# Low weight products last in every chunk, and the second block's gate products, sums and splits in another order

## The chip, the cores and the metric

One core of a Trainium2 chip runs the whole program, a single launch. The metric is the device time of that launch in microseconds. TensorE (PE) multiplies, VectorE (DVE), ScalarE (ACT) and GpSimd (POOL) work on tiles in SBUF and PSUM, and SyncE (SP) issues the DMA transfers of the weights.

## What is computed

Two blocks, each with two layers, on 256 tokens of width 1024, all in fp32. Cut to its frame:

```python
def first_block(h, ...):
    for l in range(2):
        proj = rms_norm(h, norm1_w[l]) @ w_in[l]
        z, xbc, dt_f, dt_b, sc_b, sc_c, sc_v = split(proj)
        mix = concat([ssd_branch(z, xbc, dt_f, dt_b, ...), sc_b * dwconv(sc_c * sc_v)])
        h = h + mix @ w_out[l]
        n = rms_norm(h, norm2_w[l])
        gate, up = split(dwconv(n @ w_ffn_up[l]) + ffn_conv_b[l])
        h = h + (silu(gate) * up) @ w_ffn_down[l]          # 2 x 2816 columns up
    return rms_norm(h, final_norm_w)

def second_block(x, ...):
    for l in range(2):
        u_conv, dq, dk, dv, mq, mk, mv, g = split(x @ w_in[l])
        y_a = conv_branch(u_conv, ...)           # 31-wide conv, layer norm, silu, @ w_conv_out
        y_b = diff_attention(dq, dk, dv, ...)    # ... @ w_diff_out
        y_c = moba_attention(mq, mk, mv, ...)    # ... @ w_moba_out
        gates = sigmoid(g + b_gate[l])
        m = gates[0] * y_a + gates[1] * y_b + gates[2] * y_c
        x = layer_norm(alpha * x + m @ w_o[l], ...)
        h = relu(x @ w_ff1[l] + b_ff1[l]) ** 2   # 4096 columns
        x = layer_norm(alpha * x + h @ w_ff2[l] + b_ff2[l], ...)
    return x
```

## The kernel before

Every large product is fp32 made of three products of rounded parts (fp32r): a weight is `whi + wlo`, an input `xh + xl`, and the kernel adds whi·xh, whi·xl and wlo·xh in PSUM. The weights are cut into chunks of 1 MB (half as much in a few). SP loads chunk after chunk into `raw`, which has three slots. ScalarE rounds it into `whi` in two halves (`split_hi`, L1095, semaphore `hi_done`); it first waits until the chunk two before has been multiplied (`chunk_done`). VectorE subtracts, again in two halves (`split_lo`, L1527, semaphore `w_ready`), and TensorE multiplies.

Three kinds of chunk matter. A *plain* chunk (`gemm`, L504 to L506) has 48 products of 256 columns: for every tile of weights the three products stand in a row. A *wide* chunk (the FFN's way up, `gemm_wide`, L549 and L550) has 16 pairs: one product of 512 columns, whi with both input parts side by side, and one of 256, wlo with the high input part. A *down* chunk (`down_pass`, L607 to L609, and its like for the mix's and the attention's way out, L579 to L581) has 24 products of 512 columns, in which the weights stream and the hidden tile stands: high × high, high × low weights, low hidden × high weights, again three in a row into one PSUM bank. In the FFNs a down chunk stands behind two wide ones in the first block and behind one in the second. `weights(c, cx, half)` waits for `w_ready` of that half ahead of its first product of any kind.

In front of each of the four layers' two matrix stages stands a norm. Its result comes out tile by tile: ScalarE writes the high part (L1147), VectorE the low one (L1616, L1605 in the first block), and the first chunk behind the norm takes the tiles as they come (`gemm_paced`, or `gemm_wide` with `base`), waiting for `n_ready`, the low part, of each. Down chunks wait for `hid_ready`, the low part of the hidden tile (L1876 in the first block).

In the second block chunks 28 to 31 are the outputs of the diff-attention and conv branches and chunks 32 to 35 those of the MoBA branch. VectorE multiplies each with its gate out of PSUM (`gated`, L2070; L2101 in the loop over q), GpSimd adds the products of chunks 30 and 31 into `macc` (L1073, two SBUF inputs), VectorE adds those of 32 to 35 (L2103), ScalarE halves and rounds the sum (L1481) and VectorE makes its low part (L2107), the input of chunks 36 and on (L579 to L581, w_o). Each engine has one queue in program order, and this order is written out by hand.

## Time and profile before

| | us |
|---|---|
| median of three runs | 1733.12 |
| lowest, highest | 1733.06, 1733.71 |
| the profiled execution, its own time | 1733.45 |
| its span in the trace | 1731.6 |
| TensorE busy | 1698.5 (98%) |
| VectorE busy | 1331.9 (77%) |
| ScalarE busy | 961.3 (56%) |
| GpSimd busy | 60.2 (3%) |

The granted TensorE clock has a mean of 0.998 of full speed. Busy time is a share of the span; the matmuls overlap, so one of 256 columns has a record of 0.28 us though the next begins 0.12 us after it. What a product costs is therefore read from the distance of starts, and where TensorE stands still from its list of waits. A row of the timeline has the start, the duration (of all in a folded row), engine, line, operation and tiles, and in brackets the idle time ahead and who ended it.

### The profile page before, as it was taken

The numbers are of one execution on the slowest core, as the hardware profiler recorded it, in microseconds if no ns is written. First come the engines' busy times: TensorE is split into PE (matmuls) and PEld (weight loads), VectorE is DVE, ScalarE is ACT, GpSimd is POOL, SyncE is SP. The second block draws the span as 40 slices with busy tenths as digits, with TensorE's granted clock in tenths as the row PEclk, the third lists the DMA queues.
The fourth block names the chain that finished last, engine by engine and source line by source line (L and its number), as shares of the span: only waits on it lengthen the run. The fifth ranks groups of instructions, "written<-read, shape, count | busy, mean of one in ns | idle before, by whom it ended". The sixth has DMA issues, their size and how long they took to land.

```text
span 1731.6 us, 27884 instructions
## 1 busy us (share of the span) xinstructions
PE 1698.5 (98%) x11152; PEld 1514.4 (87%) x11152; DVE 1331.9 (77%) x2074; ACT 961.3 (56%) x1584; POOL 60.2 (3%) x81
## 2 busy tenths in 40 slices
PE   8999999999999999999999999999999999999998
PEld 7999888888999988888899998788879999978886
DVE  6867678888877758878799888766678988886666
ACT  5566556565656656655645654544454476454443
POOL 1000000000200000000000001000000000100001
PEclk9999999999999999999999999999999999999999
DMA  7544545555545446555466454555546645455552
GB/s 217 164 146 147 170 163 182 191 194 158 171 146 148 146 160 204 195 187 184 162 199 194 147 171 150 197 185 188 193 149 216 195 146 172 135 194 195 192 186 84
DMA packets 233006, 299.71 MB, mean 173 GB/s; under 512 B 6163, under 2 KB 198317, under 8 KB 232877
## 3 DMA queue, kind: packets, MB, share of 16 engines
q1 hardware_dynamic: 232569, 297.82, 53.2%
q8 instruction: 88, 1.44, 0.3%
q14 instruction: 41, 0.34, 0.1%
q10 hardware_dynamic: 308, 0.12, 0.0%
HBM read 292.67 MB, written 1.05 MB: 170 GB/s over the span
## 4 chain that ended last, share of the span: by engine, by line
PE 82%; DVE 13%; ACT 2%; issue 2%; POOL 0%; DVEq 0%; ACTq 0%; POOLq 0%
PE ring_banks L549 16%; PE ring_banks L504 9%; PE ring_banks L505 9%; PE ring_banks L506 9%; PE ring_banks L550 8%; PE bank L607 5%; PE bank L608 5%; PE bank L609 5%; DVE weights_lo L1527 5%; PE ring_banks L579 2%; PE ring_banks L581 2%; PE ring_banks L580 2%; PE bank L729 1%; DVE conv_sums L1933 1%; PE ring_banks L634 1%
## 5 line engine op out<-in xcount | busy, mean ns | idle before, releaser
L1527 DVE TENSOR_TENSOR weights_lo<-raw_weights,weights_hi 128x1024 fp32r<-128x1024 f32 (+1 forms) x552 | 648.3, 1215 | 115.5 <-ACT weights_hi L1095 114.3
L1095 ACT ACTIVATE weights_hi<-raw_weights 128x1024 fp32r<-128x1024 f32 (+1 forms) x552 | 544.3, 1037 | 201.8 <-PE bank L609 95.1
L504 PE MATMUL ring_banks<-input_parts,weights_hi 128*128 128x256 f32 x1568 | 450.5, 287 | 10.3 <-DVE weights_lo L1527 4.0
L505 PE MATMUL ring_banks<-input_parts,weights_hi 128*128 128x256 f32 x1568 | 444.2, 283 | 0.0
L506 PE MATMUL ring_banks<-input_parts,weights_lo 128*128 128x256 f32 x1568 | 444.1, 283 | 0.0
L549 PE MATMUL ring_banks<-input_parts,weights_hi 128*128 128x512 f32 x1184 | 420.3, 398 | 4.0 <-DVE input_parts L1616 3.3
L550 PE MATMUL ring_banks<-input_parts,weights_lo 128*128 128x256 f32 x1184 | 332.0, 280 | 0.0
L504 PEld LDWEIGHTS ring_banks<-input_parts,weights_hi 128*128 128x128 f32 x1568 | 301.1, 192 | 16.0 <-issue 13.3
L505 PEld LDWEIGHTS ring_banks<-input_parts,weights_hi 128*128 128x128 f32 x1568 | 301.3, 192 | 0.1
L506 PEld LDWEIGHTS ring_banks<-input_parts,weights_lo 128*128 128x128 f32 x1568 | 301.2, 192 | 0.0
L549 PEld LDWEIGHTS ring_banks<-input_parts,weights_hi 128*128 128x128 f32 x1184 | 222.3, 188 | 60.2 <-issue 3.7
L550 PEld LDWEIGHTS ring_banks<-input_parts,weights_lo 128*128 128x128 f32 x1184 | 223.5, 189 | 1.8
L607 PE MATMUL bank<-weights_hi,hidden_hi 128*128 128x512 f32 x432 | 169.4, 392 | 1.1 <-DVE hidden_lo L1876 1.1
L608 PE MATMUL bank<-weights_lo,hidden_hi 128*128 128x512 f32 x432 | 168.6, 390 | 0.0
L609 PE MATMUL bank<-weights_hi,hidden_lo 128*128 128x512 f32 x432 | 168.4, 390 | 0.0
L1933 DVE SCALAR_TENSOR_TENSOR conv_sums<-conv_padded,params_second_layer,conv_sums 128x256 f32<-128x256 f32 x240 | 98.8, 478 | 0.0
L607 PEld LDWEIGHTS bank<-weights_hi,hidden_hi 128*128 128x128 f32 x432 | 81.1, 188 | 19.9 <-DVE hidden_lo L1876 1.9
L609 PEld LDWEIGHTS bank<-weights_hi,hidden_lo 128*128 128x128 f32 x432 | 81.1, 188 | 17.8
L608 PEld LDWEIGHTS bank<-weights_lo,hidden_hi 128*128 128x128 f32 x432 | 81.1, 188 | 15.1
L1495 ACT ACTIVATE pair<-ring_banks,params_second_layer 128x256 f32<-128x256 f32 x64 | 26.9, 471 | 106.2 <-PE ring_banks L550 106.2
L2139 DVE TENSOR_TENSOR pair<-ring_banks,pair 128x512 f32<-128x512 f32 x32 | 22.1, 691 | 75.7 <-ACT pair L1495 75.7
L579 PE MATMUL ring_banks<-weights_hi,hidden_hi 128*128 128x512 f32 x192 | 75.9, 395 | 1.5 <-DVE weights_lo L1527 1.5
(272 smaller groups left out, 2161.6 us busy)
## 6 DMA issues: line engine op xcount, KB each, us to landing
raw_weights<-in_w_in SPq DMA_DIRECT2D x104, 1024.0 KB, 5.3
raw_weights<-in_w_ff SPq DMA_DIRECT2D x64, 1024.0 KB, 5.3
raw_weights<-in_w_ffn_up SPq DMA_DIRECT2D x44, 1024.0 KB, 5.0
raw_weights<-in_w_ffn_down SPq DMA_DIRECT2D x22, 1024.0 KB, 4.9
raw_weights<-in_w_out SPq DMA_DIRECT2D x16, 1024.0 KB, 5.1
raw_weights<-in_w_o SPq DMA_DIRECT2D x8, 1024.0 KB, 5.1
pair<-pair SPq DMA_DIRECT2D x64, 64.0 KB, 2.8
raw_weights<-in_w_diff_out SPq DMA_DIRECT2D x4, 1024.0 KB, 5.1
```

Of the source, the lines that this page charges most:

```text
L504: mm(o, w_hi, x_hi, start=first, stop=False, skip_group_check=quiet)
L505: mm(o, w_hi, x_lo, start=False, stop=False, skip_group_check=quiet)
L506: return mm(o, w_lo, x_hi, start=False, stop=last, skip_group_check=quiet)
L549: mm(b[:, :], wh, inputs[:, k, :, :].rearrange("p a t -> p (a t)"), start=first, stop=last, skip_group_check=True)
L550: return mm(b[:, 0:SEQ], wl, nh[:, k, :], start=False, stop=last, skip_group_check=True)
L579: mm(banks[t][:, :], x_h, w_h, start=opens and k == 0, stop=False)
L607: mm(o, x_h, whi[:, s, r], start=first, stop=False)
L608: mm(o, x_h, wlo[:, s, r], start=False, stop=False)
L609: return mm(o, x_l, whi[:, s, r], start=False, stop=last)
L1095: A(whi[:, t, i * n:(i + 1) * n], raw[:, s, i * n:(i + 1) * n], ACT.Copy).then_inc(hi_done, 1)
L1527: tt(wlo[:, t, r], raw[:, s, r], whi[:, t, r].bitcast(f32), SUB).then_inc(w_ready, 1)
L1933: ins = stt(out=cacc[:, k, :], in0=src, scalar=w, in1=cacc[:, k, :], op0=MUL, op1=ADD)
```

## The change

In every chunk the products with high weights now come first and wait for `hi_done` only; those with low weights follow and wait for `w_ready`. In a plain chunk that is 32 products, then 16. A wide chunk has its 16 products of 512 columns, then its 16 of 256. A down chunk has 8 of high × high (waiting for `hid_hi`, the hidden tile's high part), 8 of low hidden × high weights (`hid_ready`), and 8 with low weights; consecutive products go to different banks. At a norm the first chunk waits for `n_hi`, and the products of the low input part stand two tiles behind; a wide chunk at a norm becomes 48 products of 256 columns. SP's queue is as before.

In the second block `gate_product` of chunk 30's first half moves between the two conv activations. The products of chunk 31 go to two further buffers, and GpSimd's sums wait for `chunk_done` of chunk 31 (m = 0, 1) and 32 (m = 2, 3). VectorE waits for the sums' first half ahead of the q loop and for the rest at q = 2. The low split of chunk 36 is cut in two around q2's product, that of chunk 37 stands ahead of q3's product (it stood behind it), and ScalarE splits chunk 37 ahead of its wait for q3's sum.

```diff
-            def passes(o, w_hi, w_lo, x_hi, x_lo, first, last, quiet=False):
-                mm(o, w_hi, x_hi, start=first, stop=False, skip_group_check=quiet)
-                mm(o, w_hi, x_lo, start=False, stop=False, skip_group_check=quiet)
-                return mm(o, w_lo, x_hi, start=False, stop=last, skip_group_check=quiet)
-            def weights(c, cx, half):
+            def high(c, cx, half):
+                pe.wait_ge(hi_done, cx * 2 + (2 * c + half + 1))
+            def low(c, cx, half):
                 pe.wait_ge(w_ready, (cx + c) * 2 + (2 * RAW + 1 + half))
...
+            def add(o, w, x, first=False, last=False):
+                return mm(o, w, x, start=first, stop=last, skip_group_check=True)
+            def gemm(c, cx, u, ux, o, nk, n, xh, xl, x0=0):
                 if u is not None:
                     pe.wait_ge(ring_free, ux + u + 1)
...
+                for i in range(2):
+                    high(c, cx, i)
+                    for m in range(n // P):
+                        for k in range(i * nk // 2, (i + 1) * nk // 2):
+                            wh, wl = tile(c, k * n + m * P)
+                            add(target(m), wh, xh[:, x0 + k, :], k == 0 and m % 2 == 0)
+                            add(target(m), wh, xl[:, x0 + k, :])
+                for i in range(2):
+                    low(c, cx, i)
+                    for m in range(n // P):
+                        for k in range(i * nk // 2, (i + 1) * nk // 2):
+                            wh, wl = tile(c, k * n + m * P)
+                            last = add(target(m), wl, xh[:, x0 + k, :], False, k == nk - 1)
                 last.then_inc(chunk_done, 1)
...
+            def gemm_paced(c, cx, freed, left, right, base):
+                pe.wait_ge(ring_free, freed)
+                def by_low_input(i):
+                    k = TRANSPOSED[i]
                     pe.wait_ge(n_ready, base + (i + 1))
                     for m in range(2):
                         wh, wl = tile(c, k * 256 + m * P)
+                        last = add(right[m], wh, nl[:, k, :], False, i == 7)
+                    return last
+                for i, k in enumerate(TRANSPOSED):
+                    if i % 4 == 0:
+                        high(c, cx, i // 4)
+                        low(c, cx, i // 4)
+                    pe.wait_ge(n_hi, base + (i + 1))
+                    for m in range(2):
+                        wh, wl = tile(c, k * 256 + m * P)
+                        add(left[m], wh, nh[:, k, :], i == 0 and (m == 0 or right is not left))
+                        add(left[m], wl, nh[:, k, :])
+                    if i >= 2:
+                        by_low_input(i - 2)
+                by_low_input(6)
+                by_low_input(7).then_inc(chunk_done, 1)
+            def gemm_wide(c, cx, freed, v):
+                pe.wait_ge(ring_free, freed)
+                for i in range(2):
+                    high(c, cx, i)
+                    for m in range(2):
+                        for k in range(4 * i, 4 * i + 4):
+                            wh, wl = tile(c, k * 256 + m * P)
+                            add(wide_bank(v, m), wh, inputs[:, k, :, :].rearrange("p a t -> p (a t)"), k == 0)
+                for i in range(2):
+                    low(c, cx, i)
+                    for m in range(2):
+                        for k in range(4 * i, 4 * i + 4):
+                            wh, wl = tile(c, k * 256 + m * P)
+                            last = add(wide_bank(v, m)[:, 0:SEQ], wl, nh[:, k, :], False, k == 7)
                 last.then_inc(chunk_done, 1)
...
+            def wide_paced(c, cx, freed, v, base):
+                parts = [[wide_bank(v, m)[:, i * SEQ:(i + 1) * SEQ] for m in range(2)] for i in range(2)]
+                gemm_paced(c, cx, freed, parts[0], parts[1], base)
...
+                def by_high(k, t):
+                    o, x_h, x_l, w_h, w_l = parts(k, t)
+                    add(o, x_h, w_h, opens and k == 0)
+                    add(o, x_l, w_h)
+                if first_tokens is None:
+                    for i in range(2):
+                        high(c, cx, i)
+                        for t in range(TOK):
+                            by_high(2 * i, t)
+                            by_high(2 * i + 1, t)
+                    for i in range(2):
+                        low(c, cx, i)
+                        for t in range(TOK):
+                            by_low(2 * i, t)
+                            last = by_low(2 * i + 1, t)
...
+            def down(c, cx, t0, opens, n):
+                places = [(t, half) for t in range(TOK) for half in range(2)]
+                pe.wait_ge(hid_hi, n)
                 for kk in range(2):
...
+                    high(c, cx, kk)
+                    for t, half in places:
+                        o, x_h, x_l, w_h, w_l = down_parts(c, t0, kk, t, half)
+                        add(o, x_h, w_h, opens and kk == 0)
+                pe.wait_ge(hid_ready, n)
+                for kk in range(2):
+                    for t, half in places:
+                        o, x_h, x_l, w_h, w_l = down_parts(c, t0, kk, t, half)
+                        add(o, x_l, w_h)
+                for kk in range(2):
+                    low(c, cx, kk)
+                    for t, half in places:
+                        o, x_h, x_l, w_h, w_l = down_parts(c, t0, kk, t, half)
+                        last = add(o, x_h, w_l)
+                last.then_inc(chunk_done, 1)
+            def down_last(c, cx, t0, n):
+                pe.wait_ge(hid_hi, n)
+                for kk in range(2):
+                    high(c, cx, kk)
+                    for half in range(2):
+                        o, x_h, x_l, w_h, w_l = down_parts(c, t0, kk, 0, half)
+                        add(o, x_h, w_h)
...
                     pool.wait_ge(ring_free, l * U2 + (UB2 + U2_OUT + 4 + m + RING + 1))
+                    if m % 2 == 0:
+                        pool.wait_ge(chunk_done, l * C2 + (CB2 + 31 + m // 2 + SPL + 1))
                     x = macc[:, 2 * m:2 * m + 2, :]
-                    nc.gpsimd.tensor_tensor(x, x, tmp[m % 2][:], ALU.add).then_inc(pool_added, 1)
+                    product = tmp[(0, 1, 3, 4)[m]]
+                    nc.gpsimd.tensor_tensor(x, x, product[:], ALU.add).then_inc(pool_added, 1)
...
                         split_hi(34 + q, cx, cr, columns(list2, 34 + q))
+                    else:
+                        split_hi(37, cx, cr)
                     act.wait_ge(mp_ready, l * 4 + q + 1)
                     A(hidh[:, 2 * q:2 * q + 2, :], macc[:, 2 * q:2 * q + 2, :], ACT.Copy, scale=0.5).then_inc(mp_hi, 1)
-                split_hi(37, cx, cr)
...
+                def gate_product(c, m):
+                    first = c < 30
+                    j = c - 28 if first else c - 30
+                    u = U2_OUT + 2 * (c - 28) + m
+                    k = 4 * j + 2 * m
+                    g = gates[:, (8 if first else 16) + k:(10 if first else 18) + k, :]
+                    o = macc[:, k:k + 2, :] if first else tmp[m + 3 * j][:]
+                    stt(out=o, in0=g, scalar=1.0, in1=pair(ring[u % RING]), op0=ADD, op1=MUL).then_inc(ring_free, 1)
                 def gated(c):
                     multiplied(c, cx)
                     for m in range(2):
+                        gate_product(c, m)
                     split_lo(c + 2, cx, n=columns(list2, c + 2))
                 gated(28)
                     x = cacc[:, 2 * q:2 * q + 2, :]
                     dve.wait_ge(cth, l * 2 + q + 1)
                     stt(out=x, in0=tmp[3 + q][:], scalar=1.0, in1=x, op0=ADD, op1=MUL).then_inc(cact, 1)
+                    if q == 0:
+                        multiplied(30, cx)
+                        gate_product(30, 0)
                 for q in range(2):
                     dve.wait_ge(chi, l * 2 + q + 1)
                     t = slice(8 + 2 * q, 10 + 2 * q)
                     tt(hidl[:, t, :], cacc[:, 2 * q:2 * q + 2, :], hidh[:, t, :].bitcast(f32), SUB).then_inc(conv_ready, 1)
-                gated(30)
+                gate_product(30, 1)
+                split_lo(32, cx, n=columns(list2, 32))
+                dve.wait_ge(cact, l * 2 + 2)
+                gated(31)
                 dve.wait_ge(pool_added, l * 4 + 2)
-                gated(31)
-                dve.wait_ge(pool_added, l * 4 + 4)
                 for q in range(4):
                     c, u = 32 + q, U2_OUT + 8 + q
                     multiplied(c, cx)
+                    if q == 2:
+                        split_lo(36, cx, halves=(0,))
+                        dve.wait_ge(pool_added, l * 4 + 4)
+                    if q == 3:
+                        split_lo(37, cx)
                     x = macc[:, 2 * q:2 * q + 2, :]
                     stt(out=tmp[q % 2][:], in0=gates[:, 2 * q:2 * q + 2, :], scalar=1.0, in1=pair(ring[u % RING]), op0=ADD, op1=MUL).then_inc(ring_free, 1)
                     dve.wait_ge(ring_free, ux + (u + RING + 1))
                     tt(x, x, tmp[q % 2][:], ADD).then_inc(mp_ready, 1)
-                    if q < 3:
+                    if q < 2:
                         split_lo(c + 2, cx, n=columns(list2, c + 2))
+                    if q == 2:
+                        split_lo(36, cx, halves=(1,))
                     dve.wait_ge(mp_hi, l * 4 + q + 1)
                     stt(out=hidl[:, 2 * q:2 * q + 2, :], in0=x, scalar=0.5, in1=hidh[:, 2 * q:2 * q + 2, :].bitcast(f32), op0=MUL, op1=SUB).then_inc(mp_split, 1)
-                split_lo(37, cx)
```

TensorE in the FFN of the first block, where two wide chunks end and a down chunk begins. Before (one row for each product; `input_parts` is the norm's result, `bank` an accumulator of the down chunks):

```order
L549 MATMUL ring_banks<-input_parts,weights_hi 128x512
L550 MATMUL ring_banks<-input_parts,weights_lo 128x256
L549 MATMUL ring_banks<-input_parts,weights_hi 128x512
L550 MATMUL ring_banks<-input_parts,weights_lo 128x256
L607 MATMUL bank<-weights_hi,hidden_hi 128x512
L608 MATMUL bank<-weights_lo,hidden_hi 128x512
L609 MATMUL bank<-weights_hi,hidden_lo 128x512
L607 MATMUL bank<-weights_hi,hidden_hi 128x512
```

and now, from a down chunk's end on, two wide chunks and the next down chunk (×16 is 16 products in a row):

```order
L516 MATMUL bank<-weights_hi,hidden_lo 128x512 x8
L516 MATMUL bank<-weights_lo,hidden_hi 128x512 x8
L516 MATMUL ring_banks<-input_parts,weights_hi 128x512 x16
L516 MATMUL ring_banks<-input_parts,weights_lo 128x256 x16
L516 MATMUL ring_banks<-input_parts,weights_hi 128x512 x16
L516 MATMUL ring_banks<-input_parts,weights_lo 128x256 x16
L516 MATMUL bank<-weights_hi,hidden_hi 128x512 x8
L516 MATMUL bank<-weights_hi,hidden_lo 128x512 x8
L516 MATMUL bank<-weights_lo,hidden_hi 128x512 x8
```

The products of 512 and of 256 columns no longer alternate, and in the down chunk the low hidden part and the low weights have moved behind all of high × high.

VectorE in the second block's gate stretch, from the second conv activation on. Before (`pair` is a product's buffer, `queries_keys` the sum `macc`):

```order
L2088 SCALAR_TENSOR_TENSOR conv_sums<-pair,conv_sums 128x512 x2
L2092 TENSOR_TENSOR hidden_lo<-conv_sums,hidden_hi 128x512 x2
L2070 SCALAR_TENSOR_TENSOR pair<-gates,ring_banks 128x512 x2
L1527 TENSOR_TENSOR weights_lo<-raw_weights,weights_hi 128x512 x2
L2070 SCALAR_TENSOR_TENSOR pair<-gates,ring_banks 128x512 x2
L1527 TENSOR_TENSOR weights_lo<-raw_weights,weights_hi 128x512 x2
L2101 SCALAR_TENSOR_TENSOR pair<-gates,ring_banks 128x512
L2103 TENSOR_TENSOR queries_keys<-queries_keys,pair 128x512
L1527 TENSOR_TENSOR weights_lo<-raw_weights,weights_hi 128x512 x2
L2107 SCALAR_TENSOR_TENSOR hidden_lo<-queries_keys,hidden_hi 128x512
```

Before, from q2 on:

```order
L2101 SCALAR_TENSOR_TENSOR pair<-gates,ring_banks 128x512
L2103 TENSOR_TENSOR queries_keys<-queries_keys,pair 128x512
L1527 TENSOR_TENSOR weights_lo<-raw_weights,weights_hi 128x1024 x2
L2107 SCALAR_TENSOR_TENSOR hidden_lo<-queries_keys,hidden_hi 128x512
L2101 SCALAR_TENSOR_TENSOR pair<-gates,ring_banks 128x512
L2103 TENSOR_TENSOR queries_keys<-queries_keys,pair 128x512
L2107 SCALAR_TENSOR_TENSOR hidden_lo<-queries_keys,hidden_hi 128x512
L1527 TENSOR_TENSOR weights_lo<-raw_weights,weights_hi 128x1024 x2
```

Now, of the same stretch's beginning:

```order
L2171 SCALAR_TENSOR_TENSOR conv_sums<-pair,conv_sums 128x512
L2147 SCALAR_TENSOR_TENSOR pair<-gates,ring_banks 128x512
L2171 SCALAR_TENSOR_TENSOR conv_sums<-pair,conv_sums 128x512
L2178 TENSOR_TENSOR hidden_lo<-conv_sums,hidden_hi 128x512 x2
L2147 SCALAR_TENSOR_TENSOR pair<-gates,ring_banks 128x512
L1605 TENSOR_TENSOR weights_lo<-raw_weights,weights_hi 128x512 x2
L2147 SCALAR_TENSOR_TENSOR pair<-gates,ring_banks 128x512 x2
L1605 TENSOR_TENSOR weights_lo<-raw_weights,weights_hi 128x512 x2
```

Now, from q2 on:

```order
L1605 TENSOR_TENSOR weights_lo<-raw_weights,weights_hi 128x1024
L2193 SCALAR_TENSOR_TENSOR pair<-gates,ring_banks 128x512
L2195 TENSOR_TENSOR queries_keys<-queries_keys,pair 128x512
L1605 TENSOR_TENSOR weights_lo<-raw_weights,weights_hi 128x1024
L2201 SCALAR_TENSOR_TENSOR hidden_lo<-queries_keys,hidden_hi 128x512
L1605 TENSOR_TENSOR weights_lo<-raw_weights,weights_hi 128x1024 x2
L2193 SCALAR_TENSOR_TENSOR pair<-gates,ring_banks 128x512
L2195 TENSOR_TENSOR queries_keys<-queries_keys,pair 128x512
L2201 SCALAR_TENSOR_TENSOR hidden_lo<-queries_keys,hidden_hi 128x512
```

One product has moved ahead of the second activation, and the splits of chunks 36 and 37 (128x1024) stand around and ahead of the last two products of L2193, where two stood behind the one and two at the end.

## Rows read from the trace of the kernel before

**Rows 1.** TensorE on the page: busy us, share, instructions

```profile
PE 1698.5 (98%) x11152; PEld 1514.4 (87%) x11152; DVE 1331.9 (77%) x2074; ACT 961.3 (56%) x1584; POOL 60.2 (3%) x81
```

**Rows 2.** TensorE's waits: line, releaser, us in total, times, longest

```profile
PE ring_banks L504 <- DVE weights_lo L1527: 7.6, 13, 1.0
PE ring_banks L549 <- DVE input_parts L1616: 3.3, 4, 0.9
PE ring_banks L504 <- DVE input_parts L1616: 3.1, 3, 1.5
PE ring_banks L504 <- DVE input_parts L1605: 3.0, 2, 2.5
...
PE ring_banks L579 <- DVE weights_lo L1527: 1.5, 4, 0.6
...
PE bank L607 <- DVE hidden_lo L1876: 1.1, 2, 0.5
```

**Rows 3.** Timeline of TensorE: start us, us, engine, line, tiles

```profile
225.43 0.39 PE L579 MATMUL ring_banks<-weights_hi,hidden_hi 128*128 128x512 f32 x1
...
230.87 0.39 PE L579 MATMUL ring_banks<-weights_hi,hidden_hi 128*128 128x512 f32 x1
...
246.65 0.39 PE L549 MATMUL ring_banks<-input_parts,weights_hi 128*128 128x512 f32 x1
...
252.19 0.39 PE L549 MATMUL ring_banks<-input_parts,weights_hi 128*128 128x512 f32 x1
...
268.77 0.39 PE L549 MATMUL ring_banks<-input_parts,weights_hi 128*128 128x512 f32 x1
...
285.56 0.39 PE L549 MATMUL ring_banks<-input_parts,weights_hi 128*128 128x512 f32 x1
...
1117.99 0.39 PE L549 MATMUL ring_banks<-input_parts,weights_hi 128*128 128x512 f32 x1
...
1129.10 0.39 PE L549 MATMUL ring_banks<-input_parts,weights_hi 128*128 128x512 f32 x1
```

**Rows 4.** Timeline, first block's plain chunks, TensorE and VectorE

```profile
26.88 0.36 PE L504 MATMUL ring_banks<-input_parts,weights_hi 128*128 128x256 f32 x1 [0.76 <-DVE weights_lo L1527]
...
459.04 0.35 PE L504 MATMUL ring_banks<-input_parts,weights_hi 128*128 128x256 f32 x1 [0.64 <-DVE weights_lo L1527]
...
25.51 2.36 DVE L1527 TENSOR_TENSOR weights_lo<-raw_weights,weights_hi 128x1024 fp32r<-128x1024 f32 x2 [4.48 <-ACT weights_hi L1095]
```

**Rows 5.** Timeline of TensorE, last down chunk of layer 0

```profile
420.67 0.50 PE L607 MATMUL bank<-weights_hi,hidden_hi 128*128 128x512 f32 x1 [0.53 <-DVE hidden_lo L1876]
```

**Rows 6.** Timeline, second block's gate stretch: GpSimd, VectorE, TensorE

```profile
1055.05 2.99 POOL L1073 TENSOR_TENSOR queries_keys<-queries_keys,pair 128x512 f32<-128x512 f32 x2 [13.34 <-DVE pair L2070]
...
1055.49 3.10 DVE L1527 TENSOR_TENSOR weights_lo<-raw_weights,weights_hi 128x512 fp32r<-128x512 f32 x2
...
1062.73 0.68 DVE L2101 SCALAR_TENSOR_TENSOR pair<-gates,ring_banks 128x512 f32<-128x512 f32 x1
...
1064.05 1.29 DVE L1527 TENSOR_TENSOR weights_lo<-raw_weights,weights_hi 128x512 fp32r<-128x512 f32 x2
...
1068.98 0.68 DVE L2101 SCALAR_TENSOR_TENSOR pair<-gates,ring_banks 128x512 f32<-128x512 f32 x1
...
1073.18 0.68 DVE L2101 SCALAR_TENSOR_TENSOR pair<-gates,ring_banks 128x512 f32<-128x512 f32 x1
...
1075.28 0.69 DVE L2107 SCALAR_TENSOR_TENSOR hidden_lo<-queries_keys,hidden_hi 128x512 fp32r<-128x512 f32 x1 [0.70 <-ACT hidden_hi L1481]
...
1077.60 0.47 PE L579 MATMUL ring_banks<-weights_hi,hidden_hi 128*128 128x512 f32 x1 [0.21 <-DVE weights_lo L1527]
```

**Rows 7.** Timeline at the second block's FFN norm, TensorE and VectorE

```profile
1099.54 0.47 PE L549 MATMUL ring_banks<-input_parts,weights_hi 128*128 128x512 f32 x1 [0.87 <-DVE input_parts L1616]
...
1099.87 0.43 DVE L1616 TENSOR_TENSOR input_parts<-pair,input_parts 128x256 fp32r<-128x256 f32 x1 [0.48 <-ACT input_parts L1147]
```

**Rows 8.** Start of the program: stretch, us, busy (count), PEclk, DMA

```profile
16.70:20.10 3.40, 3.40 (x18) 3.40 (x17) 3.16 (x6) 2.35 (x6) 0.81 (x2) 0.51 0.34 64
```

164 lines of the change are left out of this document (65 added, 99 removed).

## The prediction

> **What bounds the kernel now.** I read the page first: TensorE is busy for 98% of the span [rows 1], so only two things can save time, its idle gaps and the pitch (start to start) of its matmuls. The waits of TensorE come next [rows 2]: VectorE's low weight parts hold it 7.6 us in 13 waits at L504 and 1.5 us at L579, the split of a norm's result (L1616, L1605) 3.3, 3.1 and 3.0 us in nine waits, the low part of a hidden tile 1.1 us. A gap costs more than its idle time: a record of 0.28 us normally overlaps its successor, which starts 0.12 later, so 0.16 of it comes into view ahead of a gap; and the first product behind one is longer, 0.36 [rows 4]. I add 0.16 + 0.07 = 0.23 us for each gap.
>
> The pitches are read from starts [rows 3]. Where nothing disturbs it, a stream of 512-column products runs at (230.87 − 225.43)/24 = 0.2267 us. The wide chunks of the FFN alternate one of 512 and one of 256: (252.19 − 246.65)/16 = 0.347 a pair, which leaves 0.120 for one of 256. Between down chunks the pair costs more: two wide chunks and a down chunk take 285.56 − 268.77 = 16.79 us, 16 times 0.347 and 24 times 0.2267 would make 5.55 + 5.55 + 5.44 = 16.54. Starts inside such a triple show the down chunk's first ten products at 0.225 to 0.241 and 0.06 us lost by that; the other 0.19 is on the two wide chunks, 5.64 us each. In the second block a pair of one wide and one down chunk takes 1129.10 − 1117.99 = 11.11, so 5.47 for the down chunk.
>
> **A, chunks of the first block.** Before, the first product of a chunk's half needs the low weights. Now 32 high products stand ahead of the first low one. At 26.88 TensorE has waited 0.76 us for L1527, at 459.04 0.64 us [rows 4]; there are five such waits in both layers, 4.0 us in sum. VectorE began that split at 25.51, right behind the high half that it needs, so the high half lay there when TensorE came free at 26.88 − 0.76 = 26.12. The split's two halves end at 27.87; the first low product is now wanted 32 × 0.12 = 3.8 us later than the start, at about 29.9. The gap goes, and 2 us are to spare. Gain: 4.0 + 5 × 0.23 = **5.2 us**. What is late next is the high half itself, and ScalarE is the less busy engine.
>
> **B, the last down chunk of the first block's FFN.** TensorE waits at 420.67 for the low hidden part [rows 5], and the high part is what that operation subtracts, so it is older by the whole operation. The new order starts on it: 1.1 + 2 × 0.23 = **1.6 us** in both layers [rows 2].
>
> **C, the gate chunks of the second block.** Here VectorE is the late one, and GpSimd makes it late [rows 6]: the two splits at 1055.49 take 3.10 us while GpSimd adds from 1055.05 for 2.99; two of the same size take 1.29 at 1064.05 without it. This occurs twice in a layer, so the stretch holds 2 × 1.81 = 3.6 us of held splits. TensorE's waits on L1527 in it are 7.6 − 4.0 = 3.6 us at L504 and 1.5 us at L579 in both layers, six gaps in each (0.21 at 1077.60 is the last): 5.1 + 12 × 0.23 = 7.9, so 3.95 us in a layer if all go. Not all can. VectorE's chain goes on: q0 and q1 take 1068.98 − 1062.73 = 6.25, q2 with a whole split 1073.18 − 1068.98 = 4.20, and the split of chunk 37, 2.36 us, now stands ahead of q3's product, where it stood behind. Without the held splits q0 starts at 1062.73 − 3.6 = 1059.1; then q3's product starts at 1059.1 + 6.25 + 4.2 + 2.4 = 1071.9, and its last operation, which TensorE needs for chunk 37, ends as before (1075.28 + 0.69 − 1073.18) = 2.8 later, at 1074.7. GpSimd's sums now start with chunk 31's end, beside q0 and q1. There they meet a split or two of 0.6 us; I add 0.6. Chunk 37 then starts at 1075.3 in place of 1077.60: **2.3 us a layer, 4.6 in all**. That is a new wait in place of six old ones, on q3's low part instead of on a weight split. ScalarE now splits chunk 37 before it rounds q3's sum, 2 us of work that it needs to have started by about 1071; behind it are only that sum and the wait of TensorE for it. Since ScalarE is busy 56% of the span, I count nothing, and up to 1 us a layer if the split is late. Bounds: if the products that read PSUM are held by GpSimd too, I put another 1.95 us, and 0.35 a layer is left; with no contact 3.95.
>
> Which bound is nearer depends on who holds whom. In this trace VectorE's split, with both inputs in SBUF, is held, as the row at 1055.49 shows. The Trainium skill (SBUF — State Buffer, "SBUF: two separate sides") says that VectorE and GpSimd share a port pair as an exclusive lock for a whole instruction, contended by a VectorE operation with two SBUF inputs and a GpSimd operation that reads SBUF. By it a product with one input in PSUM is not held, and the sum stays at 4.6; were it wrong in this, C would be 0.7.
>
> **D, the eight norm boundaries.** The waits on L1616 and L1605 are 3.3 + 3.1 + 3.0 = 9.4 us [rows 2]. Now TensorE goes on with the high input part alone, and needs the low one two tiles later. What stood between the two is the subtraction L1616, 0.43 us; at 1099.54 TensorE waited 0.87 us [rows 7], at most half of which is then left. With nine waits shortened by 0.45 that is 4.1, and four of them vanish with their 0.23: +0.9. Against it, the four wide chunks at a boundary now run 48 products of 256 columns, 48 × 0.120 = 5.76, where 16 pairs took 5.55 to 5.64: −0.7 in all. **4.3 us**. Ends: 2.5, if a boundary is bound by the transposes ahead of both parts, and 8, if nearly all waits go.
>
> **E, the streams of the FFN.** Wide chunks now run 16 products of 512 and then 16 of 256 instead of pairs: 16 × 0.2267 + 16 × 0.120 = 5.55 us. That is no gain against the undisturbed pair, 5.547, and one of 0.09 against the pair between down chunks. A 512 stream that follows 256s needs some ten products to reach 0.2267 (down chunks between wide ones show it, and it costs 0.05). A triple then takes 5.55 + 5.60 + 5.50 = 16.65 (the second wide chunk pays the 0.05), gain 0.14, a pair 5.55 + 5.47 = 11.02, gain 0.09. First block: nine triples in a layer, less 0.1 for its first four chunks, 1.2; second block: 14 pairs in a layer, 1.3. **5.0 us** in all. Ends: nothing in a row shows a long 512 stream between 256s, so it may stay at 0.235, and a chunk takes 5.68: 0.04 more, −2.8 in 70; and if it doesn't need to settle at all, +6.
>
> The down chunks' new order (high × high, high × low, low × high) computes the same 24 products and costs nothing by the pitch. What hides the later use of the low weights is only that it's later.
>
> **Sum.** 5.2 + 1.6 + 4.6 + 4.3 + 5.0 = 20.7 us. The profiled execution took 1733.45, 0.33 over the median, within the spread of the runs; the gaps are those of any run. So 1733.1 − 20.7 = **1712.4 us**.
>
> **Rivals.** (1) *The 512 streams don't settle.* E is −2.8 to 2 instead of 5: 1715 to 1720. For it: the down chunk between wide chunks needs ten products to settle, and there are no longer streams than 24 beside 256s. Against: it does settle there.
> (2) *The gaps are given back.* VectorE is busy 1331.9 of 1731.6 us; low parts come at the same times as before, and the 20 us saved must be found in its idle time. In C the PSUM products may be held, and D may be bound by the transposes: 0.7 + 2.5 with A, B, E whole is 15.0 us: 1718; with E at its end also, 1726.
> (3) *More than the sum.* D 8, C 7.9 and E 6: 28.7 us, 1704.
> (4) *Slower: the clock falls in the down chunks.* There three products in a row went to one bank, now each goes to another than the one before. If a matmul couldn't start before the bank switch was through, TensorE would idle a moment each time, and the granted clock would fall. What that costs the start shows: 18 matmuls in 3.40 us at a granted clock of 0.51, the lower of its two levels, 1.2 GHz [rows 8], 0.19 each against 0.12, so some 1.4 us for a stretch of that length. It decides from 15 such stretches (20.7/1.4) on; with one in each of the 54 down chunks of the FFNs (22 and 32) it is +76, less the gain about 1788. Against it: before, the bank changed after every third product, and the product behind such a change started as soon as any other, at 0.2267 (the 24 products between the first two starts of [rows 3]); only the kernel's very start shows the low level.
> The Trainium skill (TensorE: Matmul & The Clock Gate, "A second HAM failure mode: psum-queue depth-cycling") tells of a bf16 kernel in which cycling through PSUM banks made such pauses and the clock swung between its two levels. No row of this kernel shows that; by this rule the time would be that of rival 4.
> (5) *The change doesn't do what it says*: the low products wait as before because the high parts are as late. ScalarE is busy 56% and VectorE starts each split right behind it, so a high half is over 1 us older than its low one; I give it nothing beyond "same".
>
> **How the numbers follow.** The forecast as it stands, with its own range of 1708 to 1716: 0.60. Rival 1: 0.15. Rival 2: 0.12. Rival 3: 0.07. Rival 4: 0.03. Nothing measurable: 0.03. The range from 1705.5 to 1721 leaves out rival 4, "same", most of rival 3 and the worse half of rival 2, some 0.17. A difference of 0.2% (3.5 us) is about what a measurement of this kernel tells from none. Only rival 4 gives slower: faster 0.94, same 0.03, slower 0.03.
>
> **What would show each step.** A: no wait of a first-block matmul on the low split above 0.2 us; VectorE's splits where they were. B: the last down chunk starts behind its predecessor. C: between chunks 30 and 36 of the second block no wait on a low split, GpSimd's adds starting with chunk 31's end, and one wait of up to 1 us at chunk 37's first or second pass on L2201. D: waits of at most 0.45 us on the input's high part. E: starts 0.2267 apart in a wide chunk's first half, 0.120 in its second, and a chunk of 5.55 to 5.6 us. It would be wrong if wide chunks took over 5.64, if busy TensorE time didn't fall by about 5 us, if products of VectorE beside GpSimd took over 1 us, or if the clock left 1.00 anywhere behind the start.

## The result

The changed kernel takes 1712.65 us (median of four runs, 1712.20 to 1712.98) against 1733.32 (four runs, 1733.06 to 1733.71): a ratio of 0.988 with a 95% interval of 0.9863 to 0.9898. The forecast was 1712.4. The total was right almost to the digit, and that is in part luck: of its five terms one (E) was too small, one (D) too large, inside a third (C) two mistakes cancelled, and some 0.8 us of the gain between the two traces came from the clock at the start, of which the forecast had nothing.

The page of the changed kernel, first part:

```profile
PE 1687.9 (99%) x11216; PEld 1518.0 (89%) x11216; DVE 1329.8 (78%) x2074; ACT 960.1 (56%) x1584; POOL 60.9 (4%) x81
```

TensorE is busy 10.6 us less than in [rows 1], in a span that is 20.7 us shorter. So about half of the gain is idle time that has gone, and half is the distance of starts and the ends that show ahead of a gap. The forecast had named 5 us as the fall of busy time. TensorE's waits in the changed kernel (line, releaser: us in total, times, longest):

```profile
PE ring_banks L516 <- DVE pair L2193: 2.8, 2, 1.4
PE ring_banks L516 <- issue: 2.4, 4, 0.7
PE ring_banks L516 <- ACT input_parts L1210: 2.0, 1, 2.0
...
PE bank L718 <- DVE squares L1674: 2.0, 4, 0.8
PE ring_banks L516 <- ACT input_parts L1224: 1.7, 4, 0.5
```

Against [rows 2]: no wait on a low weight split is named any longer, nor one on a hidden tile's low part (the four of "issue", below, are for low splits all the same). There is one new wait, 1.4 us in each layer of the second block, on the product L2193. The waits behind a norm have passed from VectorE's low part to ScalarE's high part. "issue" is a wait in the middle of the norm's chunk, where VectorE's low split of the second half has just ended (1087.77 + 1.22 = 1088.99 us, TensorE's next product at 1089.08). The statistics of the norm (L1674) are waited for longer, 2.0 us where it was 1.1; both new waits stand behind the last down chunks of the first block.

The two traces can be laid side by side at the start of the last product of each of the 276 chunks. What TensorE has gained from one such point to the next, summed by part:

| part | forecast, us | the two traces, us |
|---|---|---|
| A, plain chunks of the first block | 5.2 | 3.03 − 0.26 in layer 0, 2.04 in layer 1: 4.8 |
| B, last down chunk of the first FFN | 1.6 | 0.81 + 0.81 = 1.6 |
| C, gate chunks of the second block | 4.6 | 2.15 + 2.12 = 4.3 |
| D, first chunks behind the eight norms (chunk 0: 1.1), and their successors | 4.3 | 3.7 |
| E, wide and down chunks of the four FFNs | 5.0 | 1.81 + 1.80 + 1.48 + 1.50 = 6.6 |
| sum | 20.7 | 21.0 |

The start has a scatter of its own: over the changed kernel and the eight below that share its beginning, the last product of chunk 0 starts between 21.05 and 21.85 us. So a difference of up to 0.8 us between two traced spans may be nothing but this, and small terms are read behind chunk 0.

### The profile page after: what moved, and what is told of

It is laid out like the page before. It is cut to its first block, busy times and chain, and to the rows that moved or that the text cites. A ratio compares the mean times of both kernels' runs of the same rounds, so it can differ in the third digit from the quotient of the medians.

```text
span 1710.9 us, 28028 instructions
## 1 busy us (share of the span) xinstructions
PE 1687.9 (99%) x11216; PEld 1518.0 (89%) x11216; DVE 1329.8 (78%) x2074; ACT 960.1 (56%) x1584; POOL 60.9 (4%) x81
## 4 chain that ended last, share of the span: by engine, by line
PE 87%; DVE 11%; issue 1%; ACT 1%; POOL 0%; DVEq 0%; ACTq 0%; POOLq 0%
PE ring_banks L516 64%; PE bank L516 16%; DVE weights_lo L1605 4%; PE bank L807 1%; DVE conv_sums L2011 1%; PE bank L918 1%; PE bank L929 1%; PE ring_banks L712 1%; PE bank L755 0%; PE bank L792 0%; DVE norm_statistics L1712 0%; PE bank L953 0%; PE bank L815 0%; POOL norm_small L1070 0%; PE bank L718 0%
## 5 line engine op out<-in xcount | busy, mean ns | idle before, releaser
L516 PE MATMUL ring_banks<-input_parts,weights_hi 128*128 128x256 f32 (+1 forms) x4384 | 695.5, 312 | 6.5 <-issue 2.4
L516 PEld LDWEIGHTS ring_banks<-input_parts,weights_hi 128*128 128x128 f32 x4384 | 615.7, 191 | 54.8 <-issue 9.5
L516 PE MATMUL ring_banks<-input_parts,weights_lo 128*128 128x256 f32 x2752 | 373.9, 283 | 0.0
L516 PEld LDWEIGHTS ring_banks<-input_parts,weights_lo 128*128 128x128 f32 x2752 | 355.2, 192 | 5.5
L516 PE MATMUL bank<-weights_hi,hidden_hi 128*128 128x512 f32 x432 | 110.7, 392 | 0.0
L516 PE MATMUL bank<-weights_lo,hidden_hi 128*128 128x512 f32 x432 | 109.3, 389 | 0.0
L516 PE MATMUL bank<-weights_hi,hidden_lo 128*128 128x512 f32 x432 | 109.3, 389 | 0.0
L516 PE MATMUL ring_banks<-weights_hi,hidden_lo 128*128 128x512 f32 x192 | 74.9, 390 | 0.0
L516 PE MATMUL ring_banks<-weights_lo,hidden_hi 128*128 128x512 f32 x192 | 48.7, 389 | 0.0
L516 PE MATMUL ring_banks<-hidden_hi,weights_hi 128*128 128x256 f32 x192 | 47.4, 287 | 0.0
```

The costliest lines, as they stand in the source:

```text
L516: return mm(o, w, x, start=first, stop=last, skip_group_check=True)
```

## Experiments

Each kernel is the changed one with the edit shown, unless it says otherwise. "Chunk by chunk" is the comparison of last products with the changed kernel, the scatter of chunk 0 taken off. Kernels that were measured together share their runs of the kernel before.

### E: what the wide chunks' order is worth

**wide_pairs** puts the pairs back:

```diff
 def gemm_wide(c, cx, freed, v):
-    (16 products of 512 columns, then 16 of 256)
+    for m in range(2):
+        for k in range(8):
+            if m == 0 and k in (0, 4): high(c, cx, k // 4); low(c, cx, k // 4)
+            add(wide_bank(v, m), wh, inputs of tile k, k == 0)
+            last = add(wide_bank(v, m)[:, 0:SEQ], wl, nh[:, k, :])
```

> The changed kernel with one part undone: wide chunks alternate one product of 512 and one of 256 columns again, and so wait for the low weights. If the FFN's gain of the changed kernel comes from the separate streams (the distance between the two kernels grows by 6.6 us over the wide and down chunks of the four FFNs), 1719.2 us, with the pair at 0.353 us between down chunks. If it comes from the down chunks' new order or from waits for low weights, 1713 to 1714. My forecast's own term was 5.0, which would be 1717.7.

Measured 1721.45 us (before 1733.78, ratio 0.9930, 0.9914 to 0.9947): 8.8 more than the changed kernel, more than either account. Chunk by chunk, a wide chunk between down chunks loses 0.08 or 0.11 us. In the first block the down chunk behind two of them loses another 0.03, in the second block it loses nothing. That makes 0.22 us for two wide chunks and a down chunk and 0.107 for one and one, and it is the 6.6 of the table. The other 2 us are two things. The first is in the pairs themselves. Chunks 34 to 36, which ran at 0.347 a pair before, now run at 0.353 as the rest: here a pair is not simply "undisturbed" ahead of the first down chunk. That is 0.3 us in each layer of the first block. And the wide chunk right behind a norm's chunk in the second block loses 0.79 in each layer, since its first product waits for the low split again:

```profile
1097.69 0.47 PE L516 MATMUL ring_banks<-input_parts,weights_hi 128*128 128x512 f32 x1 [0.47 <-DVE weights_lo L1603]
```

**wide_eights** and **wide_fours** ask what it is in the pairs that costs:

```diff
-for i in range(2): 8 products of 512;  for i in range(2): 8 of 256
+for m in range(2): 8 products of 512 (k = 0..7), 8 of 256            # wide_eights
+for m in range(2): for i in range(2): 4 products of 512, 4 of 256    # wide_fours
```

> The changed kernel with wide chunks in groups of eight: 8 products of 512, 8 of 256, and this again, so one more switch from 256 to 512 in each of 70 chunks. If what costs is each switch (in the changed kernel the five products behind one lose 0.036 us in sum), 70 x 0.036 = 2.5 us more, 1715.2. If groups of eight run as groups of sixteen do and only strict alternation costs, 1712.4 to 1713.0.

> The changed kernel with wide chunks in groups of four products of 512 and four of 256, in turn: three more switches to 512 in each of 74 chunks than the changed kernel. Groups of eight (one more) cost 0.020 us a chunk by the trace, strict pairs (15 more) 0.08 to 0.11. If each switch costs alike until the settled pitch is no longer reached, 3 x 0.020 x 74 = 4.4: 1717. If the cost has saturated at that of the pairs, 7: 1720. If groups of four still settle for nothing more than eights, 1.5: 1714.

wide_eights: 1714.03 us (before 1733.78, ratio 0.9888, 0.9873 to 0.9902); chunk by chunk +0.020 in each wide chunk, 1.4 in all. wide_fours: 1716.89 (before 1733.28, ratio 0.9906, 0.9891 to 0.9921); the spans differ by 4.19, less 0.16 at chunk 0, 4.0 in the 72 wide chunks that are not at a norm (42 and 30; the expectations count 70 and 74), 0.056 for each. Laid on the second block's wide chunk with its down chunk, one more switch costs 0.020 us, three more 0.067, fifteen more 0.107; on the first block's two wide chunks with theirs, two more cost 0.040, six more 0.113, thirty more 0.22. So a switch from 256 to 512 columns has a price of about 0.02 us, and from four products to single ones it saturates, at 0.007 a switch. The starts show both. Behind a switch in the changed kernel they are 0.233, 0.236, 0.228, 0.233 and 0.230 us apart before they settle at 0.227, 0.026 in excess, and the two short first 256s (0.114 and 0.119 for 0.120) give 0.007 of it back. Strict pairs never settle: their 512s are 0.232, 0.241 and 0.236 apart and their 256s 0.118, 0.120 and 0.113, in a cycle. The price by count of switches accounts for E; why a switch costs anything, no run shows. My price of a switch was 0.05, for ten products, and the changed kernel needs five. The triple and the pair of [rows 3] in the changed kernel:

```profile
264.71 0.39 PE L516 MATMUL ring_banks<-input_parts,weights_hi 128*128 128x512 f32 x1
...
281.29 0.39 PE L516 MATMUL ring_banks<-input_parts,weights_hi 128*128 128x512 f32 x1
...
1103.55 0.39 PE L516 MATMUL ring_banks<-input_parts,weights_hi 128*128 128x512 f32 x1
...
1114.55 0.39 PE L516 MATMUL ring_banks<-input_parts,weights_hi 128*128 128x512 f32 x1
```

16.58 us in place of 16.79, and 11.00 in place of 11.11.

**down_old** puts three products in a row to one bank again in all down chunks but the last of each FFN:

```diff
 def down(c, cx, t0, opens, n):
-    (8 high x high; wait hid_ready, 8 low hidden; wait low weights, 8 with them)
+    pe.wait_ge(hid_ready, n)
+    for kk in range(2): high(c, cx, kk); low(c, cx, kk)
+        for t in range(TOK): for half in range(2): add high x high, x_h x w_l, x_l x w_h
```

> The changed kernel with the down chunks (all but the last of each FFN) in the order before, three products in a row to one bank, and their old waits. If the change of bank at every product costs or gives nothing, 1712.4 to 1713.0. In the traces a down chunk of the first block gained 0.03 us and one of the second lost 0.01, which would make 1713.1. If rotating the banks costs clock or time that hid other gains, it is faster by 1 us or more.

Measured 1713.74 us (before 1733.09, ratio 0.9889, 0.9875 to 0.9904), 1.1 more. Chunk by chunk, 0.47 and 0.43 of it stand at the first down chunk of each second-block FFN, where the hidden tile's low part is late:

```profile
1098.83 0.50 PE L516 MATMUL bank<-weights_hi,hidden_hi 128*128 128x512 f32 x1 [0.16 <-DVE hidden_lo L2232]
```

All other down chunks are equal to 0.02 us. The bank that changes at every product costs nothing, and the granted clock of the changed kernel is 1.00 from 20.10 to 1700 us (stretch, busy us and count of PE, PEld, DVE, ACT, POOL, PEclk, DMA share, GB/s):

```profile
20.10:1700.00 1679.90, 1669.77 (x11124) 1507.13 (x11123) 1311.23 (x2035) 950.01 (x1565) 53.62 (x66) 1.00 0.54 175
```

That is the end of rival 4. The Trainium skill (TensorE: Matmul & The Clock Gate, "A second HAM failure mode: psum-queue depth-cycling") tells of a bf16 kernel whose clock swung while it cycled through PSUM banks, with small pauses between its groups of products. In this kernel the banks change without pauses (0.2267 us a product) and the clock does not swing.

### A: the plain chunks

**plain_old**: the first block's plain chunks, all but those at a norm, with three products in a row and low weights waited for first.

```diff
-gemm(c, cx, u, ux, [ring[u % RING]], 8, 256, nh, nl)
+gemm(c, cx, u, ux, [ring[u % RING]], 8, 256, nh, nl, old=True)   # and the 128-column chunk
```

> The changed kernel with the first block's plain chunks (all but those at a norm) in the order before, three products in a row, low weights waited for first. By the two traces the new order gave 0.99 + 1.17 + 0.87 us in layer 0, 0.26 of it given back at the eighth chunk, and 1.18 + 0.86 in layer 1, 4.8 in all: 1717.5 us; my forecast's term was 5.2: 1717.9. If TensorE's gain there is bound anyway by the vector work of the mixer, 1713 to 1715.

Measured 1717.47 us (before 1733.28, ratio 0.9909, 0.9892 to 0.9925). Chunk by chunk the steps come back one by one: 0.99, 1.17, 0.87, then 0.26 the other way at the eighth chunk, and 1.17 and 0.87 in layer 1; 4.7 in all. VectorE's splits stand as they did. The 0.26 at the eighth chunk is a new, short wait of TensorE ahead of it: its first product on `diagonals` starts 0.30 us behind the chunk's last product, where it was 0.12, since ScalarE has written that tile only at 54.33 us (the product starts at 54.47). The first of these gaps in the changed kernel:

```profile
24.88 0.28 PE L516 MATMUL ring_banks<-input_parts,weights_hi 128*128 128x256 f32 x1
...
24.43 2.36 DVE L1605 TENSOR_TENSOR weights_lo<-raw_weights,weights_hi 128x1024 fp32r<-128x1024 f32 x2 [3.17 <-ACT weights_hi L1172]
```

Against [rows 4]: TensorE no longer waits for the split that takes until 26.79; it starts 1.9 us ahead of its end.

### C: what the gate stretch waits for

The changed kernel, VectorE and GpSimd beside each other, and what holds TensorE:

```profile
1045.40 6.43 POOL L1150 TENSOR_TENSOR queries_keys<-queries_keys,pair 128x512 f32<-128x512 f32 x4 [15.20 <-PE ring_banks L516]
```

```profile
1045.36 1.29 DVE L2147 SCALAR_TENSOR_TENSOR pair<-gates,ring_banks 128x512 f32<-128x512 f32 x2 [0.71 <-PE ring_banks L516]
1046.57 2.39 DVE L1605 TENSOR_TENSOR weights_lo<-raw_weights,weights_hi 128x512 fp32r<-128x512 f32 x2
1048.88 0.67 DVE L2193 SCALAR_TENSOR_TENSOR pair<-gates,ring_banks 128x512 f32<-128x512 f32 x1
1049.59 1.08 DVE L2195 TENSOR_TENSOR queries_keys<-queries_keys,pair 128x512 f32<-128x512 f32 x1
1050.59 2.38 DVE L1605 TENSOR_TENSOR weights_lo<-raw_weights,weights_hi 128x512 fp32r<-128x512 f32 x2
...
1060.89 2.36 DVE L1605 TENSOR_TENSOR weights_lo<-raw_weights,weights_hi 128x1024 fp32r<-128x1024 f32 x2
1063.17 0.68 DVE L2193 SCALAR_TENSOR_TENSOR pair<-gates,ring_banks 128x512 f32<-128x512 f32 x1
```

```profile
1063.90 0.50 PE L516 MATMUL ring_banks<-weights_hi,hidden_hi 128*128 128x512 f32 x1 [1.39 <-DVE pair L2193]
```

The second split of each held pair by itself, and a sum of GpSimd:

```profile
1047.17 1.78 DVE L1605 TENSOR_TENSOR weights_lo<-raw_weights,weights_hi 128x512 fp32r<-128x512 f32 x1
1048.37 1.75 POOL L1150 TENSOR_TENSOR queries_keys<-queries_keys,pair 128x512 f32<-128x512 f32 x1
1050.59 1.78 DVE L1605 TENSOR_TENSOR weights_lo<-raw_weights,weights_hi 128x512 fp32r<-128x512 f32 x1
```

Three things are to be seen. A product with an input in PSUM is not held by GpSimd (1.29 for two, 0.67 for one, as without it); that was the forecast. Three operations of VectorE with two SBUF inputs that start while GpSimd adds are held: one split of each of two pairs by 1.1 us (1.78 for 0.68) and the addition L2195 by 0.4, 2.6 us in a layer, where I had put 0.6. Each of them ends 0.55 us behind the end of the GpSimd addition that it met (the one from 1048.37 ends at 1050.12, L2195 at 1050.67), and the split that starts 0.1 us ahead of one, at 1046.57, isn't held. The rule of the Trainium skill (SBUF — State Buffer, "SBUF: two separate sides"), an exclusive lock for a whole instruction between a GpSimd operation that reads SBUF and a VectorE operation with two SBUF inputs, agrees in all of this. The third thing: chunk 37 does not wait for the low part of q3's sum. It waits for q3's *product*, 2.1 us earlier in that chain, because the product frees the PSUM bank into which chunk 37 is to write. (Chunks 28 to 31 are the diff-attention and MoBA outputs; 32 to 35, whose input is the activated conv tile of L2178, are those of the conv branch. "The kernel before" has the last two the wrong way round; nothing here hangs on it.)

**q3_first** moves one step:

```diff
                     if q == 3:
-                        split_lo(37, cx)
                     (product and sum of q)
+                    if q == 3:
+                        split_lo(37, cx)
```

> The changed kernel with one step moved: VectorE's product and sum of q3 stand ahead of chunk 37's low split, not behind it. If chunk 37 waits for the PSUM bank which q3's product frees, its wait of 1.39 us (with the ends 1.55) goes in both layers, and the low split is still in time: 1709.5 us. If the low split of chunk 37 then comes late, the wait only changes its name: 1712.0 to 1713.5.

Measured 1709.13 us (1708.92 to 1709.58; before 1733.09, ratio 0.9863, 0.9848 to 0.9878), the fastest kernel of the study. Chunk by chunk it is equal up to chunk 37, which gains 1.71 us in layer 0 and 1.70 in layer 1. TensorE in it at that place, and VectorE:

```profile
1061.98 0.84 PE L516 MATMUL ring_banks<-weights_lo,hidden_hi 128*128 128x512 f32 x3
1062.66 0.39 PE L516 MATMUL ring_banks<-weights_hi,hidden_hi 128*128 128x512 f32 x1
```

```profile
1061.12 0.68 DVE L2191 SCALAR_TENSOR_TENSOR pair<-gates,ring_banks 128x512 f32<-128x512 f32 x1
1061.83 0.69 DVE L2193 TENSOR_TENSOR queries_keys<-queries_keys,pair 128x512 f32<-128x512 f32 x1
1062.44 2.35 DVE L1605 TENSOR_TENSOR weights_lo<-raw_weights,weights_hi 128x1024 fp32r<-128x1024 f32 x2
```

The split now ends at 1064.79, 2.1 us into the chunk, and chunk 37 wants its first half after 16 × 0.227 = 3.6. The high-first order of TensorE had made the early split needless, and the change put it in the way.

**gates_old** keeps TensorE's new order and gives VectorE, GpSimd and ScalarE their old one in this stretch; **gates_old_dve** leaves only ScalarE's step (split of chunk 37 ahead of the wait for q3's sum) new; **gates_alone** is the kernel before with these three engines' new order and TensorE's old one.

```diff
-(gate_product(30, 0) between the activations; tmp[3], tmp[4]; sums behind chunks 31, 32;
- split_lo(36) in halves around q2, split_lo(37) ahead of q3)
+gated(30); dve.wait_ge(pool_added, l * 4 + 2)
+gated(31); dve.wait_ge(pool_added, l * 4 + 4)
+(q loop with split_lo(c + 2) for q < 3, split_lo(37) behind it)
...
-                    else:
-                        split_hi(37, cx, cr)          # gates_old only: behind the loop again
```

> The changed kernel with VectorE's, GpSimd's and ScalarE's order in the second block's gate stretch as before; only TensorE's order in it is new. If the order of products alone takes most of the gaps, the chunk 37 starts when ScalarE has its high half, behind q3's sum, at 1076.2 in the time of the kernel before, in place of 1077.60: a gain of 1.4 us a layer where the changed kernel has 2.1, so 1714.1 us. If the reordering of the other engines is what gives, the 4.3 us of the stretch are lost: 1716.9.

> As gates_old, but ScalarE splits chunk 37 ahead of its wait for q3's sum, as in the changed kernel. If chunk 37 waits for the PSUM bank that q3's product frees (as the trace of the changed kernel has it), it starts with chunk 36's end at 1074.4 in the time of the kernel before, 3.2 us a layer: 1710.5, less than the changed kernel. If it waits for q3's low part, as my forecast had it, it starts at 1076.0: 1713.7.

> The kernel before with the second block's new order of VectorE, GpSimd and ScalarE alone; TensorE's order is the old one. Undoing these three in the changed kernel cost 1.9 us of the stretch's 4.3. If the two parts add up, this gives 1.9: 1731.2 us (against 1733.1). If either alone removes most of the gaps and the other then finds little left, it gives 3 to 4: 1729 to 1730. If VectorE's chain is already late and the new order of splits makes chunk 37 wait for q3's product from an earlier start, it gives under 1: 1732 to 1733.

gates_old: 1714.65 us (before 1733.78, ratio 0.9891, 0.9876 to 0.9906). Against the kernel before, the stretch still gains 1.24 us in layer 0 and 1.23 in layer 1 (expected 1.4), and TensorE waits for ScalarE:

```profile
1065.02 0.47 PE L516 MATMUL ring_banks<-weights_hi,hidden_hi 128*128 128x512 f32 x1 [1.45 <-ACT weights_hi L1169]
```

gates_old_dve: 1711.63 us (ratio 0.9873, 0.9858 to 0.9887). Its chunk 37 gains the same 1.71 and 1.70 us on the changed kernel as that of q3_first, since here q3's product has no split ahead of it; but at chunk 33 it loses 1.10, where TensorE waits (0.8 us at the longest) for a split that GpSimd has held:

```profile
PE ring_banks L516 <- DVE weights_lo L1602: 1.7, 2, 0.8
```

```profile
1047.96 3.10 DVE L1602 TENSOR_TENSOR weights_lo<-raw_weights,weights_hi 128x512 fp32r<-128x512 f32 x2
```

That is what the new order of VectorE and GpSimd gives once TensorE has its own, without its early split: q3_first is 0.9 us a layer ahead of gates_old_dve at the stretch's end, less than the 1.7 that the early split takes. ScalarE's one step, the whole difference between gates_old and gates_old_dve, is worth 1.7 us a layer at chunk 37 (1714.65 to 1711.63 us).

gates_alone: 1730.56 us (ten runs, before 1733.28 in thirteen, ratio 0.9985, 0.9976 to 0.9994). Its ten runs go from 1729.7 to 1731.6 and the interval allows a gain of 1 to 4 us, so the stretch is read from the trace: 1.4 us in each layer. The two alone give 1.24 + 1.4 = 2.6 a layer and together 2.15, so they overlap by a fifth; neither of my first two accounts (they add up, or one is enough) holds.

### D: the first chunk behind a norm

**norm_old** gives these chunks their old waits and order, **norm_late** moves the low weight products of the second half to their end:

```diff
# norm_old
-pe.wait_ge(n_hi, base + (i + 1)); high and low weights; low input two tiles later
+pe.wait_ge(n_ready, base + (i + 1)); all three products (or the pair) of the tile
# norm_late
-    if i % 4 == 0: high(c, cx, i // 4); low(c, cx, i // 4)
+    if i % 4 == 0: high(c, cx, i // 4)
+    (low(c, cx, 0) at i == 0; low(c, cx, 1) and its 8 products behind the loop)
```

> The changed kernel with the eight first chunks behind a norm as before: both input parts and both weight parts are waited for, the wide ones run 16 pairs. The two traces give 3.7 us for these places: 1716.4. The forecast's term was 4.3: 1717.0. If TensorE only waits elsewhere in the norm stretch, 1712.7 to 1713.5.

> The changed kernel with the low weight products of the second half of the eight first chunks behind a norm moved to the end of these chunks. If the wait of 0.67 us in the middle of these chunks is for VectorE's low split of that half, it goes (0.67 + 0.16 in two wide chunks, 0.40 + 0.16 at the start, smaller ones elsewhere): 2 to 2.5 us less, 1710.4. If the input parts are just as late there, 1712.4 to 1712.9.

norm_old: 1715.33 us (before 1733.09, ratio 0.9897, 0.9881 to 0.9914). The spans differ by 3.1 us, of which 1.1 is at chunk 0; the rest is 0.28 to 0.44 at six of the other boundaries, 2.0 in all, and nothing at the layer 1 norm ahead of the first block's FFN (chunk 99). The table's 3.7 hold other things too: 1.7 us at the second chunk behind the second block's four norms, whose low split was late, less 0.8 that chunk 66 gives back (below, under B) and 0.3 in small steps.

Chunk 0 is a case of its own, and it is the clock's (stretch, busy us and count of PE, PEld, DVE, ACT, POOL, PEclk, DMA share, GB/s; norm_old, then the changed kernel):

```profile
16.80:20.20 3.40, 3.40 (x18) 3.40 (x18) 3.16 (x6) 2.35 (x6) 0.63 (x2) 0.50 0.30 64
...
16.70:20.10 3.40, 3.00 (x25) 2.83 (x25) 3.16 (x7) 2.35 (x6) 0.66 (x2) 1.00 0.22 48
```

In the traces of the three kernels with the old order there (before, gates_alone, norm_old) the granted clock falls to its lower level, 1.2 GHz, for these 3.4 us ([rows 8]), and chunk 0 takes 7.18 or 7.19 us from its first start to its last. With the new order it doesn't fall in six traces of ten, the changed kernel's among them, and the chunk takes 6.39 to 6.40; in the other four the fall begins at 14.9 to 15.9 us and it takes 7.19 to 7.28. So at the same clock the new order gives chunk 0 nothing: of its 1.1 us, 0.8 is the clock and 0.3 an earlier start, well inside the scatter. TensorE had stood still for 2.0 us (new order) or 2.5 us (old) ahead of the chunk in all thirteen; whether the new order keeps the clock up or chance does, these traces do not decide.

norm_late was a miss: 1714.06 us (before 1733.09, ratio 0.9891, 0.9876 to 0.9906), 1.4 us *slower* than the changed kernel; behind chunk 0 it is 1.3, 0.27 to 0.35 at each of the four second-block norms. The changed kernel's wait of 0.67 us in the middle of the chunk is for the low split. But without it TensorE meets the next late thing a moment later:

```profile
1090.41 0.74 PE L516 MATMUL ring_banks<-input_parts,weights_hi 128*128 128x256 f32 x4 [0.55 <-ACT input_parts L1235]
1091.32 0.38 PE L516 MATMUL ring_banks<-input_parts,weights_hi 128*128 128x256 f32 x1 [0.17 <-ACT input_parts L1235]
```

and ScalarE's tile waits for VectorE's, which stands behind the split in VectorE's queue:

```profile
1088.23 1.22 DVE L1616 TENSOR_TENSOR weights_lo<-raw_weights,weights_hi 128x1024 fp32r<-128x1024 f32 x1
1089.37 0.54 DVE L1712 TENSOR_SCALAR pair<-bank,params_second_layer 128x256 f32<-128x256 f32 x1
```

The end of the chunk is set by the last tiles of the norm, and the eight products that were moved behind them (8 × 0.12 = 0.96 us, for 0.67 of waiting) now come after that end.

## Why the prediction was right, and where it was not

**A** is right in mechanism and size: 4.8 (4.7 undone) for 5.2. The 0.4 is mostly the 0.26 us that come back at the eighth chunk, where TensorE, now earlier, meets ScalarE's `diagonals`: there the gap was handed on, as rival 2 has it.

**B** is right at the chunk itself, 0.81 in each layer for 0.8, but in layer 0 it does not last. The norm behind it hangs on VectorE, whose chain from the hidden tile's low part to its first `residual` has not moved (before, then now):

```profile
419.93 0.69 DVE L1876 TENSOR_TENSOR hidden_lo<-pair,hidden_hi 128x512 fp32r<-128x512 f32 x1
...
423.94 1.87 DVE L1901 TENSOR_TENSOR residual<-residual,bank 128x512 f32<-128x512 f32 x3
```

```profile
414.01 0.68 DVE L1954 TENSOR_TENSOR hidden_lo<-pair,hidden_hi 128x512 fp32r<-128x512 f32 x1
...
418.02 1.88 DVE L1979 TENSOR_TENSOR residual<-residual,bank 128x512 f32<-128x512 f32 x3
```

It is 4.01 us both times, filled by three halves of low splits (3.49 us). TensorE comes 0.8 us earlier to a norm that is not earlier, and waits there (0.65 us on L1674 at 423.40, where it had no such wait). In norm_old, which has B but not D, the gain of 0.81 is down to 0.03 by the end of chunk 66; the 0.48 that the changed kernel keeps there is D's. In layer 1 norm_old keeps 0.78. The norm there had also waited 0.72 us for its parameters, which pass through TensorE (L826) and now come 0.8 us earlier. So B by itself gave 0.8 us and not 1.6: I had taken each gap that goes as time that goes, and in layer 0 VectorE's queue was the next late thing.

**C** has the right sum by two wrong steps. I put chunk 37 at 1075.3 in the time of the kernel before; it came at 1063.90 + 11.52 = 1075.42 (11.52 is what the chunks ahead of the stretch had gained). The step that failed first is "GpSimd's sums meet a split or two of 0.6 us": they held two splits by 1.1 us each and a sum by 0.4, 2.6 us. So q3's product started at 1063.17 + 11.52 = 1074.7, not 1071.9. The step that failed second is "its last operation, which TensorE needs for chunk 37": TensorE needs the product alone, 0.7 us behind its start and not 2.8. I had 1071.9 + 0.6 + 2.8, and it was 1074.7 + 0.7: two steps that are each over 2 us off, with opposite signs. That the sum came out is luck. Had I read in the code which semaphores stand ahead of the chunk (`ring_free` of two banks and `mp_split` of the first two sums), I would have seen that the early split of chunk 37 only delays the bank, and that is the 3.4 us (1.7 in each layer, by the traces) by which q3_first beats the changed kernel. Nor was 3.95 a layer the bound with no contact: by my own chain, 1074.7 without the 0.6, it was 2.9.

That a product with a PSUM input isn't held was forecast and holds.

**D**: 4.3 was too much. I shortened nine waits by the subtraction's 0.43 us, as if each tile came on its own. The tiles come from one chain through VectorE and ScalarE, whose queue also holds the low split of the second half, and the chunk cannot end before the last tile. By norm_old the waits gave 2.0 us at six boundaries, none at a seventh, and chunk 0's 1.1 is the clock and the scatter of the start; the late low splits behind the norms gave 1.7 that I had not counted. norm_late shows that this further reordering within the chunk only costs.

**E**: 5.0 was too little, and the upper end of 6 too; it measured 6.6. The term that was mis-sized is the settling, 0.05 us over ten products (0.06 in the down chunk): it is 0.02 net in either. And pairs in the changed surroundings cost even more than before, as the chunks ahead of the first down chunk show in wide_pairs.

**The rivals.** The 512 streams do settle (1). VectorE doesn't hand the gaps back (2), except at the norm behind layer 0's FFN, and ScalarE hands back 0.26. The clock doesn't fall in the down chunks (4); its price there, 1.4 us for a stretch, should have been 3.40 − 18 × 0.12 = 1.2, which changes nothing. But the clock did move at the very start, the one place where [rows 8] had shown it low, and the sum had no term for that. Rival 3's mechanism, that C gives more, is true of q3_first (3.8 us a layer) and not of this kernel.
